# SwiGLU and retention norms: statistics behind the fourth weight unit, squares on ScalarE

## The reference

```python
def rmsnorm(x, g):
    xf = x.astype(jnp.float32)
    y = xf * lax.rsqrt(jnp.mean(xf * xf, axis=-1, keepdims=True) + RMS_EPS) * g.astype(jnp.float32)
    return y.astype(x.dtype)

def swiglu(h, w_gu, w_down):
    gu = h @ w_gu
    g, u = gu[..., :D_FF], gu[..., D_FF:]
    return (jax.nn.silu(g) * u) @ w_down

    for i in range(DEPTH):
        ...                                   # a mixer, added to h
        h = h + swiglu(rmsnorm(h, ffn_norm[i]), ffn_w_gu[i], ffn_w_down[i])
```

## Time and profile before

| | |
|---|---|
| median of 3 runs | 2397.86 us (2397.48 to 2401.97) |
| the profiled execution | 2400.79 us, span 2399.0 us |
| TensorE matmul | 2247.3 us, 94% |
| VectorE | 1222.0 us, 51% |
| ScalarE | 798.3 us, 33% |
| GpSimd | 532.7 us, 22% |
| granted TensorE clock, mean | 0.971 |
| DMA | 198.27 MB, 83 GB/s on the mean |

### The profile page before, as it was taken

The page is one execution under the profiler, slowest core; times in us unless marked ns, Lnnn a source line. Parts: engine busy times, 40 slices in busy tenths (PEclk is TensorE's granted clock), DMA queues, the critical chain, the costliest instruction groups (busy, mean ns, idle before and its releaser), DMA issues.

```text
span 2399.0 us, 26711 instructions
## 1 busy us (share of the span) xinstructions
PE 2247.3 (94%) x10598; PEld 1801.3 (75%) x10598; DVE 1222.0 (51%) x1987; ACT 798.3 (33%) x1334; POOL 532.7 (22%) x355
## 2 busy tenths in 40 slices
PE   7999999998899999999998999998994969999997
PEld 6788876886688888876666888887773748777876
DVE  5655556565544433554455444326858664444342
ACT  3334323442322222233432222213446423333321
POOL 2533334231410101222233011034125030000000
PEclk9999999998999999999999999999997989999999
DMA  4222221221233333332222333332331212222322
GB/s 139 88 62 80 80 80 54 71 80 45 71 97 97 97 97 98 96 97 89 71 61 72 97 97 97 98 97 79 94 91 44 79 57 88 75 75 78 93 74 76
DMA packets 84155, 198.27 MB, mean 83 GB/s; under 512 B 7216, under 2 KB 44208, under 8 KB 84032
## 3 DMA queue, kind: packets, MB, share of 16 engines
q1 hardware_dynamic: 81408, 189.62, 26.0%
q10 hardware_dynamic: 2624, 6.93, 0.9%
HBM read 194.40 MB, written 2.13 MB: 82 GB/s over the span
## 4 chain that ended last, share of the span: by engine, by line
PE 81%; DVE 9%; issue 4%; ACT 3%; POOL 3%; DMA 0%; DVEq 0%; SPq 0%; POOLq 0%; ACTq 0%
PE PS L523 49%; PE PS L567 5%; PE PS L569 5%; PE PS L568 5%; PE PS L592 2%; PE PS L593 2%; PE PS L594 2%; PE PS L1011 1%; PE PS L640 1%; PE PS L650 1%; PE PS L664 1%; DVE WL L1554 1%; POOL SQS L1411 1%; POOL SQT L1409 1%; PE PS L879 1%
## 5 line engine op out<-in xcount | busy, mean ns | idle before, releaser
L1554 DVE TENSOR_TENSOR WL<-WR,WH 128x1024 fp32r<-128x1024 f32 x353 | 475.2, 1354 | 786.3 <-ACT WH L1046 785.6
L1046 ACT ACTIVATE WH<-WR 128x1024 fp32r<-128x1024 f32 x353 | 370.0, 1056 | 732.2 <-DMA WR<-in_ws 723.1
L523 PE MATMUL PS<-XH,WH 128*128 128x512 f32 x1024 | 406.7, 397 | 18.9 <-ACT XH L1055 10.5
L523 PE MATMUL PS<-XL,WH 128*128 128x512 f32 x1024 | 402.3, 393 | 0.0
L523 PE MATMUL PS<-XH,WL 128*128 128x512 f32 x1024 | 402.0, 393 | 0.0
L523 PEld LDWEIGHTS PS<-XH,WH 128*128 128x128 f32 x1024 | 195.0, 190 | 65.1 <-issue 20.4
L567 PE MATMUL PS<-XH,WH 128*128 128x512 f32 x544 | 224.1, 412 | 5.0 <-DVE WL L1554 3.6
L523 PEld LDWEIGHTS PS<-XL,WH 128*128 128x128 f32 x1024 | 194.9, 190 | 41.6 <-issue 1.7
L523 PEld LDWEIGHTS PS<-XH,WL 128*128 128x128 f32 x1024 | 194.5, 190 | 41.2
L569 PE MATMUL PS<-XH,WL 128*128 128x512 f32 x544 | 214.6, 395 | 0.0
L568 PE MATMUL PS<-XL,WH 128*128 128x512 f32 x544 | 214.1, 393 | 0.0
(11 more groups left out here) (332 smaller groups left out, 3771.5 us busy)
## 6 DMA issues: line engine op xcount, KB each, us to landing
WR<-in_ws SPq DMA_DIRECT2D x281, 512.0 KB, 3.6
WR<-in_ws SPq DMA_DIRECT2D x144, 256.0 KB, 3.2
B_CB<-gates ACTq DMA_DIRECT2D x8, 512.0 KB, 3.9
XTOK<-in_x SPq DMA_DIRECT2D x2, 1024.0 KB, 8.3
out<-OUT SPq DMA_DIRECT2D x4, 512.0 KB, 2.6
R_D<-in_decay ACTq DMA_DIRECT2D x4, 256.0 KB, 2.6
GAIN<-in_post ACTq DMA_DIRECT2D x1, 512.0 KB, 5.4
CST<-in_cst SPq DMA_DIRECT2D x1, 320.0 KB, 3.4
```

Source lines behind the costliest of these rows:

```text
L523: mm = pe.matmul(PS[:, bank + o, :], l, r, start=first and kk == 0 and i == 0, stop=last and kk == 1 and i == 2)
L1046: nc.scalar.activation(WH[:, s, :], WR[:, s, :], ACT.Copy).then_inc(hi_ready, 1)
L1554: tt(WL[:, s, :], WR[:, s, :], WH[:, s, :].bitcast(F32), ALU.subtract).then_inc(lo_ready, 1)
```

## The change

The statistics matmul moves behind the fourth unit of the first group, in both feed-forward blocks and in retention. In the feed-forward blocks it writes the last bank of the other four in place of the first, in retention the third and fourth as before. TensorE's wait for the variance moves from in front of the second group to in front of the first matmul into the bank that holds the statistics. ScalarE and VectorE split eight units before they turn to the variance, not six. `variance` reads one bank where it needs only one.

In the feed-forward blocks alone, ScalarE squares the eight tiles of R (`square_x`, four behind each four `build_x` tiles) into F_SQ, which lies where HL is later; GpSimd only adds (`squares_added`). In retention GpSimd still squares.

```diff
@@ -132,7 +132,9 @@
         a = Arena()
         HH = a("HH", [P, FT, T], F32R)
+        low_at = a.at
         HL = a("HL", [P, FT, T], F32R)
+        F_SQ = sb("F_SQ", [P, DT, T], at=low_at)
         F_G = a("F_G", [P, 2, T])
         F_U = a("F_U", [P, 2, T])
         F_S = a("F_S", [P, 2, T])
@@ -502,7 +504,7 @@
         @block.tensor
         def _(pe):
-            def unit(u, kpair, hi, lo, bank, first, last, stationary, ready=None):
+            def unit(u, kpair, hi, lo, bank, first, last, stationary, ready=None, free=None):
                 s = u % RING
                 pe.wait_ge(lo_ready, u + 1)
@@ -511,6 +513,8 @@
                     if ready is not None:
                         ready(k)
                     for o in range(4):
+                        if free is not None and first and kk == 0:
+                            free(o)
                         if stationary:
                             cols = slice(kk * T + o * P, kk * T + (o + 1) * P)
                             pairs = [(WH[:, s, cols], hi[:, k, :]), (WH[:, s, cols], lo[:, k, :]),
@@ -527,10 +531,10 @@
             def stationary_x(t, k, o):
                 return t[:, k, o * P:(o + 1) * P]
-            def group(u, kpairs, hi, lo, bank, stationary=True, ready=None, between=None):
+            def group(u, kpairs, hi, lo, bank, stationary=True, ready=None, between=None, free=None):
                 for j in range(kpairs):
-                    unit(u + j, j, hi, lo, bank, j == 0, j == kpairs - 1, stationary, ready)
+                    unit(u + j, j, hi, lo, bank, j == 0, j == kpairs - 1, stationary, ready, free)
                     if between is not None and j in between:
                         between[j]()
@@ -731,17 +735,23 @@
                     for e in SPOT.get((6, 8 + 2 * q + kk), ()):
                         attend(e)
+            def variance_read(o, count):
+
+                def wait(bank):
+                    if bank == o:
+                        pe.wait_ge(rb_var, count)
+                return wait
+
             def swiglu(layer, v, s):
                 f, dn = U[f"F{layer}"], U[f"D{layer}"]
                 first = 4 * layer
                 for j in range(11):
                     n = 11 * layer + j
-                    if j == 1:
-                        pe.wait_ge(rb_var, s + 1)
                     if j >= 2:
                         pe.wait_ge(u_ready, n - 1)
                     group(f + 4 * j, 4, XH, XL, first if j % 2 == 0 else 4 - first, ready=x_ready(v),
-                          between=None if j else {1: lambda: statistics(s, 4 - first)})
+                          between=None if j else {3: lambda: statistics(s, 7 - first)},
+                          free=variance_read(3, s + 1) if j == 1 else None)
                 pe.wait_ge(u_ready, 11 * layer + 10)
                 def hidden(k):
@@ -988,12 +998,11 @@
                 own, other = own_banks(h), 4 - own_banks(h)
                 group(u, 4, XH, XL, own, ready=x_ready(7),
-                      between={1: lambda: outputs_turned(h - 1)} if h else {1: lambda: statistics(7, 6, (0,))})
-                pe.wait_ge(rb_var, 8)
+                      between={1: lambda: outputs_turned(h - 1)} if h else {3: lambda: statistics(7, 6, (0,))})
                 if h:
                     pe.wait_ge(yl_ready, 4 * h)
                     pe.wait_ge(yh_ready, 4 * h)
-                group(u + 4, 4, XH, XL, other, stationary=False)
+                group(u + 4, 4, XH, XL, other, stationary=False, free=None if h else variance_read(2, 8))
                 pe.wait_ge(rr_step, 4 * h + 4)
                 group(u + 8, 4, XH, XL, own, stationary=False)
                 pe.wait_ge(rr_ready, 4 * h + 4)
@@ -1054,6 +1063,12 @@
                         act.wait_ge(unit_used, before)
                     nc.scalar.activation(XH[:, k, :], R[:, k, :], ACT.Copy,
                                          scale=VC[:, VEC[gain] + k:VEC[gain] + k + 1]).then_inc(x_hi, 1)
+
+            def square_x(version, squared, ks):
+
+                for k in ks:
+                    act.wait_ge(r_done, 8 * version + k + 1)
+                    nc.scalar.activation(squared[:, k, :], R[:, k, :], ACT.Square).then_inc(sq_mul, 1)
             def root(s, width=T):
                 act.wait_ge(rb_var, s + 1)
@@ -1145,10 +1160,11 @@
             for d in range(2):
                 split(ao + 8 + 2 * d + 2)
                 build_x(2, 1, "ffn0", ao + 4, range(4 * d, 4 * d + 4))
+                square_x(1, F_SQ, range(4 * d, 4 * d + 4))
             def swiglu(layer, s):
                 f, dn = U[f"F{layer}"], U[f"D{layer}"]
-                split(f + 6)
+                split(f + 8)
                 root(s)
                 for j in range(11):
                     n = 11 * layer + j
@@ -1232,6 +1248,7 @@
             for d in range(2):
                 split(bo + 8 + 2 * d + 2)
                 build_x(5, 3, "ffn1", bo, range(4 * d, 4 * d + 4))
+                square_x(3, F_SQ, range(4 * d, 4 * d + 4))
             swiglu(1, 3)
@@ -1340,7 +1357,7 @@
                 else:
                     act.wait_ge(r_done, 56)
                 act.dma_start(R_D[:, :], decay[h]).then_inc(decay_in, 16)
-                split(u + 6)
+                split(u + 6 if h else u + 8)
                 if h:
                     outputs_high(h - 1)
                 else:
@@ -1410,6 +1427,17 @@
                     pool.wait_ge(sq_mul, 8 * i + k + 1)
                     nc.gpsimd.tensor_tensor(SQS[:, :], SQS[:, :], SQT[:, :], ALU.add).then_inc(sq_sum, 1)
+            def squares_added(s, squared, i=None):
+
+                i = s if i is None else i
+                pool.wait_ge(stat_done, s)
+                for k in range(1, DT):
+                    pool.wait_ge(sq_mul, 8 * i + k + 1)
+                    if k > 1:
+                        pool.wait_ge(sq_sum, 7 * i + k - 1)
+                    so_far = squared[:, 0, :] if k == 1 else SQS[:, :]
+                    nc.gpsimd.tensor_tensor(SQS[:, :], so_far, squared[:, k, :], ALU.add).then_inc(sq_sum, 1)
+
             def residual(version):
                 return lambda k: pool.wait_ge(r_done, 8 * version + k + 1)
@@ -1457,15 +1485,15 @@
                     if ENTRIES[e][0] == "merge":
                         merge(e)
-            def swiglu(layer, s, version):
-                squares(s, R, residual(version))
+            def swiglu(layer, s):
+                squares_added(s, F_SQ)
                 for j in range(11):
                     n = 11 * layer + j
                     pool.wait_ge(gs_ready, n + 1)
                     pool.wait_ge(u_ready, n + 1)
                     nc.gpsimd.tensor_tensor(F_U[:, :, :], F_G[:, :, :], F_U[:, :, :], ALU.mult).then_inc(ht_ready, 1)
-            swiglu(0, 1, 1)
+            swiglu(0, 1)
             squares(2, R, residual(2))
             def mask(p):
@@ -1491,7 +1519,7 @@
                                 .then_inc(pn_ready, 1)
                     elif entry[0] == "mask":
                         mask(n)
-            swiglu(1, 3, 3)
+            swiglu(1, 3)
             pool.wait_ge(stat_done, 4)
             pool.wait_ge(gv_ready, 1)
@@ -1567,7 +1595,7 @@
             def variance(s, bank, width=T):
                 dve.wait_ge(stat_done, s + 1)
-                v = PS[:, bank:bank + 2, :].rearrange("p b t -> p (b t)")
+                v = PS[:, bank:bank + 1 + (width > T), :].rearrange("p b t -> p (b t)")
                 ts(RB[:, 0:width], v[:, 0:width], 1.0 / D, RMS_EPS, ALU.mult, ALU.add).then_inc(rb_var, 1)
             def rstd(s, width=T):
@@ -1793,8 +1821,8 @@
             def swiglu(layer, s):
                 f, dn = U[f"F{layer}"], U[f"D{layer}"]
                 first = 4 * layer
-                split(f + 6)
-                variance(s, 4 - first)
+                split(f + 8)
+                variance(s, 7 - first)
                 rstd(s)
                 rb2 = RB[:, 0:T].unsqueeze(1).to_broadcast([P, 2, T])
@@ -2070,7 +2098,7 @@
             x_low(7, "pre1", 7)
-            split(U["R"] + 6)
+            split(U["R"] + 8)
             variance(7, 6, T + 4)
             rstd(7, T + 4)
             dve.wait_ge(rotr_in, 32)
```

## The result

The changed kernel takes 2366.72 us (median of 4, 2363.2 to 2369.27) against 2398.64 us: ratio 0.9864, interval 0.9847 to 0.9881. The forecast was 2364, with 2359 to 2371.5 as its range. The profiled execution took 2366.93 us (span 2365.1) against 2400.79 (2399.0): 33.9 us less, where the sum said 33.7.

What follows compares the result with a forecast made beforehand. TensorE, busy 94% of the span, was taken as the bound, so only its gaps could give much. Gains of 10.3 + 12.2 + 11.2 = 33.7 us gave 2364 us against the median 2397.86; range 2359 to 2371.5.

Steps and rivals of the forecast that it cites:

- the sum: Gains of the two feed-forward blocks and retention added: 10.3 + 12.2 + 11.2 = 33.7 us, all reaching the end.
- First and second block: Feed-forward blocks: with statistics behind the fourth unit, the second group starts 10.3 us earlier in the first, 12.2 in the second.
- Retention: Retention: operands set the pace; the second group starts at 1979.78 against 1990.95, 11.2 us earlier.
- The moved wait costs nothing: TensorE's variance wait, now at one bank: slack 1.1 and 0.5 us, cost nothing, bound 0.3 us a place.
- Eight splits ahead of the variance: VectorE's variance read behind eight splits: in the second block they finish 0.4 us ahead of the statistics' end.
- rival in which unit 7's transfer is late: All three places: TensorE stops at the held bank if the transfer takes 16.3 us; not faster or slower, chance 0.02.
- the row: Profile row before the change: ScalarE starts on unit 7 3.6 us after unit 2 ends, in the first block.
- ScalarE's squares cost and bring nothing: Feed-forward blocks: cost 0, bound 0.6 us; gain taken as 0, bound 1 us. Rival that they hurt: 2367 us, chance 0.07.
- Given back in SwiGLU: Rival in SwiGLU: unit 8's split comes late, losing 3 us in each block, 2370 us; chance 0.04.
- The clock stays low in retention: Rival in retention: bursts drop TensorE to 1.2 GHz from tile 4, 7.5 us lost, 2371.5 us; chance 0.07.
- The contention of VectorE and GpSimd: GpSimd's last four adds beside VectorE's splits: period 2.2 us from the trace, against 2.5 by the skill's exclusion rule.

## Why the prediction was right

- *First and second block*: 10.3 and 12.2 us forecast, 10.3 and 12.2 measured. The wait, the slow pair and the slow matmuls behind it went, all three: of the 10.3 us the wait was 8.7, and the granted clock behind it, 0.50 before, is 1.00.
- *Retention*: 11.2 forecast, 11.8 measured. The eight one-column matmuls were sized at their duration behind a gap, 1.71 us; they took 0.95 with the clock up, 0.81 from their start to the second group's. The rest of the path was 0.2 us longer than summed.
- *The moved wait costs nothing*: right. Undone, it costs 0.79 us of idle time a place and 3.0 us by the medians (forecast: about 1 us a place).
- *Eight splits ahead of the variance*: forecast 0.4 us of slack in the second block, found 0.5; the first block, which was not worked out, is the tighter one with 0.3. The rival in which unit 7's transfer is late did not come: its split began 3.7 us behind unit 2's end in the second block (1266.60 against 1262.9), where the row had 3.6.
- *ScalarE's squares cost and bring nothing*: right, from both sides (alone 0.9992; taken out, 2365.3 against 2364.69). XL 4 had 1.9 us of slack where I had 2.1 before any delay. VectorE did begin its splits 1.0 us later (1.4 forecast), but its XL 4 took 0.75 us and not 1.50, with GpSimd idle beside it, and nearly all of the delay came back. No table load was put in for them; the last four adds took 7.2 us where I had 5.4 to 8.9. The run with more squares found the cover where the profile had it.
- *Given back in SwiGLU*: no. The ratio by the marks is 0.9857, the measured ones are 0.9864 and 0.9854. Unit 8 was ready at 652.3 (forecast 652.2).
- *The clock stays low in retention*: no, 1.00 in all of tiles 4 to 7.
- *The contention of VectorE and GpSimd*: 2.2 us was right as an upper end. An add took 2.15 us beside splits in the run with GpSimd's squares, and 1.8 on the mean in the changed kernel's last four. The contention also took half of the slack that I had given the sum without ScalarE's squares: an add sized beside an idle VectorE is no measure for one beside eight splits.

The measured 2366.72 and 2364.69 us stand 0.1% and 0.03% from the forecast 2364, within the scatter of executions; that the second is so near says no more than the first.

## What to carry to other kernels

An instruction that waits for a side computation belongs behind so much independent work of its own queue that its input is there when it comes up: here the third unit was not enough (5.8 us longer), the fourth was, and further back was not tried. The gain is the wait and, where the clock falls in it, also what is lost behind it. Read it as one distance between two marks, and check for the side computation, the operands and the reader of the result when each is there and when it is wanted. Once the wait is gone, speeding up the side computation is worth nothing there. It can be worth something elsewhere: in retention the same edit shortens the path, because it relieves the engine that sets the pace. And make the wait for a buffer as narrow as the buffer, here one bank of four.

## What was not expected of the hardware

Two gaps of TensorE of the same length, 2.77 us, in one execution: behind one the granted clock was 0.51, behind the other 1.00. In both TensorE had been busy at 1.00 before; ahead of the second one there had been a gap of 1.73 us, 11 us earlier. A gap of 2.97 us left the clock at 1.00 in the profiled execution. So a gap of 2.8 to 3 us may cost the clock or may not. The same kernel shows it too. The changed kernel has two profiled executions, of 2366.93 and 2363.19 us. Between the two feed-forward blocks, where nothing was changed, TensorE idles for 2.58 us in both, and this is what follows (windows, first execution, then second):

```profile
1141.50:1144.50 3.00, 2.75 (x7) 1.93 (x7) 0.17 (x2) 0.28 (x1) 1.68 (x3) 0.50 0.04 8
```

```profile
1141.50:1144.50 3.00, 3.00 (x17) 1.55 (x16) 0.55 (x3) 0.26 (x1) 1.26 (x2) 1.00 0.01 3
```

From the first block's start to the second's the first execution takes 631.16 us and the second 629.74, so 1.4 of the 3.7 us between them lie there. Of the changed kernel's eight executions the longest, 2369.27 us, has a mean clock of 0.976, where the seven others took 2363.19 to 2366.93 at 0.978 or 0.979; it has no profile. Gaps of 0.8 us, four in a row in retention, did not lower the clock.
